# Other byte distances between the narrow weight ring and the activations in a one-core transformer kernel

## What is computed

```python
def reference(x, ...):
    x = first_block(x, ffn1_w_gu, ffn1_w_down, w_in, ..., w_out, ffn2_w_gu, ffn2_w_down)
    return second_block(x, c_2, ..., w_in_2, ..., w_out_2, final_g_2)

proj = h @ w_in                                   # mixer: "narrow" products
gate, up = jnp.split(h @ w_gu, 2, axis=-1)        # feed-forward: "wide" products
z = h @ w_in_2[l]                                 # layers: "narrow" products
```

## Time and profile before

| | |
|---|---|
| median of 3 executions | 3107.92 us (3103.35 to 3108.51) |
| profiled execution, span from first to last instruction | 3105.2 us |
| TensorE (PE) busy | 3070.2 us, 99% |
| weight loads (PEld), beside PE | 2713.0 us, 87% |
| VectorE (DVE) | 1952.8 us, 63% |
| ScalarE (ACT) | 1447.7 us, 47% |
| GpSimd (POOL) | 1270.0 us, 41% |
| read from HBM | 655.47 MB, 212 GB/s |

### The profile page before, as it was taken

One profiled execution on the slowest core, in us unless ns is written; L12 is line 12 of the kernel. 1 busy time (PEld: TensorE's weight loads), 2 busy tenths in 40 slices (PEclk: granted clock), 3 DMA queues, 4 the chain that ended last, 5 costly groups with the idle time before them and its releaser, 6 DMA issues.

```text
span 3105.2 us, 46479 instructions
## 1 busy us (share of the span) xinstructions
PE 3070.2 (99%) x19038; PEld 2713.0 (87%) x19038; DVE 1952.8 (63%) x2398; ACT 1447.7 (47%) x1877; POOL 1270.0 (41%) x621
## 2 busy tenths in 40 slices
PE   8999999999999999999999999999999999999998
PEld 7888888888999999998888888888899998899986
DVE  5778576673323446773467667677469864589764
ACT  6444444444567545544544444344444454544444
POOL 4444444444566554584444444444610004510013
PEclk9999999999999999999999999999999999999999
DMA  7878777785776565565787778787666545565454
GB/s 230 284 245 282 260 268 268 252 283 175 218 177 181 156 168 145 150 172 195 237 270 257 273 252 276 244 290 246 191 181 190 158 142 199 166 191 178 155 166 166
DMA packets 486653, 662.74 MB, mean 213 GB/s; under 512 B 67992, under 2 KB 273544, under 8 KB 486184
## 3 DMA queue, kind: packets, MB, share of 16 engines
q1 hardware_dynamic: 480952, 655.05, 66.1%
q0 software_dynamic: 4448, 2.94, 0.4%
q10 hardware_dynamic: 1040, 1.78, 0.2%
HBM read 655.47 MB, written 2.10 MB: 212 GB/s over the span
## 4 chain that ended last, share of the span: by engine, by line
PE 97%; DVE 1%; ACT 1%; issue 0%; DMA 0%; POOL 0%; ACTq 0%; DVEq 0%
PE ps L898 36%; PE ps L826 23%; PE ps L903 18%; PE ps L832 11%; PE ps L816 2%; PE ps L857 1%; PE ps L1356 1%; PE ps L1144 1%; PE ps L1125 1%; PE ps L957 0%; PE ps L1052 0%; PE ps L1152 0%; PE ps L1182 0%; PE ps L1174 0%; PE ps L1191 0%
## 5 line engine op out<-in xcount | busy, mean ns | idle before, releaser
L777 POOL TENSOR_TENSOR split_slabs<-stage,split_slabs 128x1024 fp32r<-128x1024 f32 x296 | 749.8, 2534 | 1365.6 <-ACT split_slabs L1411 1365.6
L1411 ACT ACTIVATE split_slabs<-stage 128x1024 fp32r<-128x1024 f32 x592 | 627.6, 1062 | 903.7 <-PE ps L903 665.1
L898 PE MATMUL ps<-split_slabs,h_split 128*128 128x512 f32 x3312 | 827.1, 392 | 0.9 <-ACT split_slabs L1411 0.9
L1411 ACT ACTIVATE narrow_split_slabs<-stage 128x1024 fp32r<-128x1024 f32 (+1 forms) x440 | 461.0, 1052 | 651.2 <-PE ps L832 568.1
L826 PE MATMUL ps<-h_split,narrow_split_slabs 128*128 128x256 f32 x5856 | 748.4, 280 | 0.0
L898 PEld LDWEIGHTS ps<-split_slabs,h_split 128*128 128x128 f32 x3312 | 620.8, 188 | 133.8 <-issue 5.1
L826 PEld LDWEIGHTS ps<-h_split,narrow_split_slabs 128*128 128x128 f32 x5856 | 702.8, 188 | 15.7 <-issue 12.0
L1830 DVE TENSOR_TENSOR split_slabs<-stage,split_slabs 128x1024 fp32r<-128x1024 f32 x296 | 412.2, 1395 | 368.2 <-ACT split_slabs L1411 368.1
L777 POOL TENSOR_TENSOR narrow_split_slabs<-stage,narrow_split_slabs 128x1024 fp32r<-128x1024 f32 (+1 forms) x181 | 436.0, 2418 | 315.0 <-ACT narrow_split_slabs L1411 307.3
L1830 DVE TENSOR_TENSOR narrow_split_slabs<-stage,narrow_split_slabs 128x1024 fp32r<-128x1024 f32 x259 | 333.1, 1288 | 175.8 <-ACT narrow_split_slabs L1411 174.9
L903 PE MATMUL ps<-split_slabs,h_split 128*128 128x512 f32 x1656 | 443.0, 389 | 0.3 <-POOL split_slabs L777 0.3
(11 more groups left out here) (250 smaller groups left out, 2129.4 us busy)
## 6 DMA issues: line engine op xcount, KB each, us to landing
stage<-in_w_in SPq DMA_DIRECT2D x360, 512.0 KB, 3.7
stage<-in_ffn_w_gu SPq DMA_DIRECT2D x352, 512.0 KB, 4.8
U<-in_w_ada SPq DMA_DIRECT2D x192, 512.0 KB, 5.6
stage<-in_ffn_w_down SPq DMA_DIRECT2D x176, 512.0 KB, 5.6
stage<-in_w_out SPq DMA_DIRECT2D x96, 512.0 KB, 4.1
stage<-in_w_in SPq DMA_DIRECT2D x80, 128.0 KB, 2.9
stage<-in_w_branch_c SPq DMA_DIRECT2D x32, 192.0 KB, 3.3
stage<-in_cmp_w SPq DMA_DIRECT2D x8, 512.0 KB, 5.8
```

The costliest lines, as they stand in the source:

```text
L777: nc.gpsimd.tensor_tensor(slab_part(n, 1, size(n)), stage[:, n % RING, 0:size(n)], slab_part(n, 0, size(n)).bitcast(F32), ALU.subtract).th ...
L898: mm(ps[:, 2 * pair + T, :], stationary(kk, i)[:, T * P:(T + 1) * P], w[0][:, kk, :], start=first and kk == 0 and i == 0, stop=False)
L1411: return fn(slab_part(n, 0, size(n)), stage[:, n % RING, 0:size(n)], ACT.Copy)
```

## The change

The narrow ring's one tensor of three places becomes three tensors of one place each. They still follow one another by 8192 bytes, but start 8, 24 and 48 numbers further on: 32, 96 and 192 bytes (modulo 256) from h. The work area behind them starts 48 numbers after the end of three places in place of 16, so it and all that is placed by its start moves by 128 bytes. `OSP` goes down by 32, so that `heads_split` keeps its distance to h (0 modulo 256); `act_split` keeps its own by its formula. `merged_split` moves with the work area, from 64 to 192 bytes. No instruction is added, removed or moved, on any engine, and no wait changes.

```diff
-SHIFT = 16
+SHIFT = 48
+SLOT_AT = (8, 24, 48)
...
-QK, VN, OSP = 0, 25 * S, 48
+QK, VN, OSP = 0, 25 * S, 16
...
-        narrow_ws = over("narrow_split_slabs", [P, SPLIT_MIX, 2, SLAB], F32R, SHIFT)
+        narrow_ws = [over(f"narrow_split_slabs{k}", [P, 2, SLAB], F32R, 2 * SLAB * k + SLOT_AT[k]) for k in range(SPLIT_MIX)]
...
         def slab_part(n, which, width=SLAB):
 
-            return (ws if in_wide_ring(n) else narrow_ws)[:, slot[n], which, 0:width]
+            if in_wide_ring(n):
+                return ws[:, slot[n], which, 0:width]
+            return narrow_ws[slot[n]][:, which, 0:width]
```

## The result

The changed kernel takes 3131.29 us (median of 4, 3130.21 to 3132.12) against 3107.24 us for the kernel before on the same chip. The ratio is 1.0077 with a 95% interval of 1.0066 to 1.0089: slower by 24 us, where 13 us less were forecast.

A forecast was written before the change was run, and what follows sets the result against it. TensorE, through the spacing of its matmuls, was taken to bound the kernel; -13.2 us for the three distances and zero for the rest took 3105.2 to 3092.0 us, rounded 3094.5 us against the median; range 3086 to 3129 us.

The forecast's parts named there:

- The bound: Whole kernel: TensorE, busy 3070.2 of 3105.2 us, limits the time by how fast one matmul follows the other.
- The two paces: Narrow-form matmuls: 113.2 or 117.9 ns each, chosen anew when the stream restarts and then kept; 0.4 taken as slow.
- Code, splitting engines and transfers at zero: Same instructions and waits from the new slicing, and little to win or lose on splitting engines or transfers: zero.
- the one on the three distances: Narrow-form slab borders: changing distance returns slow streams to the fast pace, each slow stretch keeping about its first slab; -13.2 us.
- the sign that I had named against this step: Narrow form: a slow stretch running on through several borders would refute the step, even with the time as forecast.
- Slower: Narrow form, every border: the fast pace is lost, each fast stretch keeping its first slab; +18.7 us, 3127 us, chance 0.24.
- No change: Narrow form: the restart alone chooses the pace and addresses have no part; 3108 us, chance 0.25.
- A third pace: Narrow form: weight tiles at 32 or 96 bytes could cost 14 ns more per matmul; 90 us, 3198 us, chance 0.05.
- the all-slow case of 3135: Narrow form: all matmuls at 117.9 ns, 27.2 us more, or 31.7 with a share of 0.3 slow now.
- The wide form: Mixer's output projection, 384 matmuls: already at the floor, loads have twice the time to hide; zero, at most 1.8 us.
- The rule on the two ports: TensorE's separate ports for streaming operand and weights: by this rule no distance matters and the sum would be zero.

## Why the prediction was wrong

**Right.** The bound: TensorE alone, by the spacing of its matmuls; busy time grew by 22.6 of the 23.4 us, and the waits of the earlier trace rows stayed. The two paces and that they hold until other work comes between: so it is with every ring at 64 bytes throughout. Code, splitting engines and transfers at zero.

**The step that failed** is the one on the three distances: "a border disturbs the relation between the two streams, and that the stream falls back to the floor there". In the changed kernel the borders did not do this. Between two slabs at 192 bytes with no other work between them the pace stayed what it was in 27 cases of 28 in the second block, slow in 15 of them. The stretch from 2694.50 us ran on through all its borders at 117.9 to 118.3 ns, which is the sign that I had named against this step. I had set the price of new distances at nothing because the only one in the trace was 64, and in two of the three places there is no floor to fall back to: the rings at 32 and 96 bytes have no slab on it, with or without borders. The narrow form lost 21.6 us instead of gaining 13.2.

The step is not false of every ring. From 192 to 64 bytes the border did what I had predicted, 21 times out of 21. Through the place at 32 bytes, from one slab at 64 to the next, the pace was kept 34 times out of 34, and in the ring of 64, 128 and 192 the pace at 64 changed each time round. So what a border does depends on the two distances at it, and I had no row for any of them.

A simple sum comes near the result: the mean of three uniform rings is (1172.4 + 1171.3 + 1160.9) / 3 = 1168.2 us, against 1167.8 measured. The same rule gives (1151.4 + 1175.3 + 1160.9) / 3 = 1162.5 for 64, 128 and 192, measured 1162.5, and (1172.4 + 2 x 1151.4) / 3 = 1158.4 for 32, 64 and 64, measured 1156.8. Part of this is luck. In the second block of the changed kernel the places at 32, 96 and 192 have mean spacings of 118.3, 118.7 and 116.0 ns (from the fifth matmul of a slab to its last), where the uniform rings have 118.4, 118.2 and 116.5: the second place lost what the third gained. And the rule fails for 64, 192 and 192: 1157.7 against 1144.3, because there the border back to 64 gives the floor to slow streams. A uniform ring has no such border, and its sum is no price of a place in another ring.

**The rivals.** "Slower" was right in sign, and its 3127 us stood near the result, but by another mechanism: it had the border lose the floor. The rings of 32, 64 and 64 bytes and of 64 and 192 show borders that lose nothing; that of 64, 128 and 192 shows a place at 64 that loses the floor every second time. "No change" gave addresses no part in what a restart finds. The traces differ there too: in the second block the kernel before came out of other work at the floor 29 times in 46, the ring all at 192 bytes 6 times in 46. "A third pace" was the right kind of cause, and I gave it 0.05. I priced it from the first products at 14 ns for a matmul, 3198 us. The runs show 3 to 5 ns above the mean of before: (1186.2 - 1146.2) / 8784 = 4.6 ns at 0 bytes, (1172.4 - 1146.2) / 8784 = 3.0 ns at 32 (8784 is the count of the two groups). The nearest row was not near: it contained waits. A row that only holds a long stream would have served better: the slow pace of 117.9 ns lies within 2.1 ns of the slowest ring, at 120, and within 5.4 of the slowest stretch, the 123.3 ns at 48 bytes.

The top of the range, 3129, cut off the all-slow case of 3135 that my own worst bound named, and the result fell between.

**The wide form.** I took zero, because a load has twice the time to hide there, and at most 1.8 us. It costs 2.1 us over 372 matmuls, 5.6 ns each, so the bound was short as well. Hiding time did not protect it: distance did, and it had been 0. Here the runs can tell distance from place, for ring and `merged_split` both moved. The two groups together took 94.7 us with both at 64 bytes (the kernel before) and with both at 192 (the ring all at 192). They took 97.0 us with `merged_split` 64 bytes further on than the ring, with the ring at 64 (area moved by 64) as with the ring at 128. The timeline shows a slab from 1405.73 to 1408.54 us, 2.81 us, 234 ns for a matmul, where the earlier trace rows give 226.7:

```profile
1405.73 2.04 PE L901 MATMUL ps<-narrow_split_slabs,merged_split 128*128 128x512 f32 x8
...
1408.54 2.03 PE L901 MATMUL ps<-narrow_split_slabs,merged_split 128*128 128x512 f32 x8
```

**The rule on the two ports.** The Trainium skill ("TensorE: Matmul & The Clock Gate", "Step-by-step: what each phase is for") has weight loads take no read bandwidth from a running matmul, by which, as I read it, no distance would matter. Here the same instructions take 3103.5 to 3150.9 us by where their operands lie, so that reading does not hold for float32r streams of 256 columns. Whether the loads take read bandwidth, which is what the sentence speaks of, no run here shows.

**What stays open.** Which part of the memory or of TensorE makes the price was not tried; no run separates a clash in memory from one of instruction timing. In the narrow form the ring alone was moved, never `h_split`, so what is called a distance here could also be the ring's own place, modulo 256 bytes or modulo more; for 48, 60 and 80 bytes the start of the ring was also off a multiple of 32. How a border can give the floor back is not explained. What a restart chooses by is open too, beyond that its odds differ between 64 and 192 bytes: the kernel before itself spreads over 3103 to 3113 us from one execution to the next, and the rings at 64 bytes with moved areas lie within 9 us of each other. The 5.2 us of narrow sum in the run with the area alone may be such a draw.

## What to carry to other kernels

Where matmuls of 256 columns run back to back and each loads new weights, try a few distances modulo 256 bytes between the two operands: they moved this kernel by up to 1.4% with no instruction changed. Take the spacing of starts in a long stretch without other work, in one ring with one distance at a time, and then measure the mixed ring as well: borders between distances can give back the floor or lose it, and the mean of the places is only a first estimate. Do not price a new distance from the one the trace has, and when something else in the arena is moved, list every pair of operands whose distance it changes.

## What the runs showed of the hardware

Streams of 256 float32r columns with a fresh load of 128 had a floor of 113.3 ns for a matmul at 64 and 192 bytes only, of nine distances tried. There the same addresses know a second pace of 117.9 ns, chosen at a restart and kept for over 90 us. Where the ring goes from 192 to 64 bytes, a slow stream came to the floor 21 times in 21, without a restart. At 0 bytes all went at 120 ns, at 32, 96 and 128 they went at 118.4, 118.2 and 118.7 on average (spacings in the second block), and 4 bytes off the good distance of 64 cost 31.5 us of narrow sum (1182.9 - 1151.4, with the work area in the same place). For streams of 512 columns it was the reverse: 0 bytes gave the floor of 226.7 ns, and 128 bytes 5.4 ns more ((62.9 + 33.8 - 61.5 - 33.2) us over 372 matmuls).
